# A two-layer conv / attention / mixture-of-experts trunk on one core: routing tile by tile, first expert rows by one-hot products, another order of the last experts

## What is computed

```python
grp_prob = softmax(h32 @ w_grp + b_grp)              # 4 groups
grp_p, grp_idx = top_k(grp_prob, 1)
exp_logits = (h32 @ w_exp + b_exp).reshape(T, 4, 8)
sel = take_along_axis(exp_logits, grp_idx[:, :, None], axis=1)[:, 0]
top_p, top_j = top_k(softmax(sel), 2)
gates = grp_p * top_p / sum(top_p)
experts = grp_idx * 8 + top_j
...
yb[e] = (silu(xr @ w1[e]) * (xr @ w3[e])) @ w2[e]     # xr: the rows routed to expert e
x = x + (sum over the two experts of gate * y)
```

## Time and profile before

| | us |
|---|---|
| median of 3 runs | 1643.52 (1643.09 to 1645.52) |
| the profiled execution, its own time | 1641.64 |
| its span in the trace | 1639.5 |

### The profile page before, as it was taken

How to read it: one execution, slowest core, us unless ns; L and a number is a source line. 1 busy time by engine, 2 the same in 40 slices (tenths; PEclk the granted TensorE clock), 3 DMA queues, 4 the chain that set the end, 5 groups by cost and what they waited for, 6 DMA issues and landing times.

```text
span 1639.5 us, 16522 instructions
## 1 busy us (share of the span) xinstructions
PE 1389.2 (85%) x6006; PEld 631.7 (39%) x6006; DVE 449.2 (27%) x859; ACT 329.3 (20%) x638; POOL 272.6 (17%) x373
## 2 busy tenths in 40 slices
PE   6998896988888888884799999996998888888883
PEld 3443453333332232231556666544333233223231
DVE  1898424110110110110444544425111011011012
ACT  3564230110000000000444444421100000000000
POOL 3787001121111111110000000001121111111110
PEclk9999896998999999998899999996999999999997
DMA  8322046899999999999500401226899999999994
GB/s 293 93 103 103 0 154 247 362 425 426 426 427 426 426 426 424 424 375 356 204 0 1 154 1 52 103 90 264 351 409 427 426 427 426 426 417 424 415 425 193
DMA packets 62540, 473.63 MB, mean 289 GB/s; under 512 B 15800, under 2 KB 15800, under 8 KB 36512
## 3 DMA queue, kind: packets, MB, share of 16 engines
q1 hardware_dynamic: 49792, 443.63, 65.9%
q0 software_dynamic: 10400, 16.82, 2.7%
q10 hardware_dynamic: 2304, 12.58, 2.0%
HBM read 466.95 MB, written 23.33 MB: 299 GB/s over the span
## 4 chain that ended last, share of the span: by engine, by line
PE 50%; DMA 35%; DVE 7%; POOL 2%; issue 2%; ACT 2%; SPq 1%; ACTq 0%; POOLq 0%; DVEq 0%
DMA ring<-in_moe_w 33%; PE banks L1350 19%; PE banks L1460 6%; PE banks L1296 4%; PE banks L1367 4%; PE banks L1489 3%; POOL scratch L519 2%; DVE banks L892 2%; PE banks L1209 2%; PE banks L1282 2%; PE banks L1549 2%; PE banks L1504 1%; PE banks L1229 1%; DMA area<-y_dram 1%; PE banks L1313 1%
## 5 line engine op out<-in xcount | busy, mean ns | idle before, releaser
L1350 PE MATMUL banks<-ring,scratch 128*64 128x512 f32 x1984 | 493.7, 648 | 137.7 <-DMA ring<-in_moe_w 126.8
L1350 PEld LDWEIGHTS banks<-ring,scratch 128*64 128x64 f32 x1984 | 158.4, 148 | 469.4 <-issue 469.4
L1044 DVE COPY scratch<-banks 128x256 f32<-128x256 f32 x65 | 27.6, 425 | 786.9 <-PE banks L1358 786.9
L1367 PE MATMUL banks<-ring,scratch 128*64 128x512 f32 x1008 | 230.2, 598 | 3.0 <-DVE scratch L1044 3.0
L703 ACT ACTIVATE scratch<-banks 64x512 f32<-64x512 f32 x65 | 38.3, 589 | 585.5 <-PE banks L1350 585.5
L537 POOL COPY at_out<-rows_out 128x1 int32 (+1 forms) x64 | 11.7, 183 | 685.9 <-ACT scratch L707 685.9
L1460 PE MATMUL banks<-hT,ring 128*128 128x512 f32 x256 | 117.9, 604 | 0.8 <-DVE hT L846 0.8
L1209 PE MATMUL banks<-hT,ring 128*128 128x512 f32 x256 | 113.1, 601 | 5.3 <-DMA ring<-in_conv_w_in 5.3
L1367 PEld LDWEIGHTS banks<-ring,scratch 128*64 128x64 f32 x1008 | 68.1, 136 | 117.4 <-issue 110.4
L519 POOL TENSOR_TENSOR scratch<-scratch 128x512 f32<-128x512 f32 x77 | 98.0, 1274 | 23.2 <-ACT scratch L670 12.9
L707 ACT ACTIVATE scratch<-banks 128x512 f32<-128x512 f32 x65 | 38.8, 597 | 284.3 <-PE banks L1367 284.3
(11 more groups left out here) (215 smaller groups left out, 1197.4 us busy)
## 6 DMA issues: line engine op xcount, KB each, us to landing
ring<-in_moe_w SPq DMA_DIRECT2D x187, 2048.0 KB, 20.8
area<-in_moe_w SPq DMA_DIRECT2D x6, 2048.0 KB, 12.2
ring<-in_attn_w_qkv SPq DMA_DIRECT2D x6, 2048.0 KB, 17.0
ring<-in_conv_w_in SPq DMA_DIRECT2D x4, 2048.0 KB, 14.2
area<-y_dram ACTq DMA_DIRECT2D x8, 1024.0 KB, 8.0
ring<-in_conv_w_out SPq DMA_DIRECT2D x2, 2048.0 KB, 21.2
xn_dram<-area ACTq DMA_DIRECT2D x8, 512.0 KB, 2.6
hT<-in_moe_w SPq DMA_DIRECT2D x2, 2048.0 KB, 7.7
```

The source lines that it names most:

```text
L1350: last = mm(bank[2 + s][q * SLOTS:(q + 1) * SLOTS, :], xeT[s][:, j, h, :], w[:, c, :], start=c == 0, stop=c == NC - 1)
L1367: last = mm(bank[6 + s][q * SLOTS:(q + 1) * SLOTS, :], hidT[s][:, j, :], w2c[:, j, q * 512:(q + 1) * 512], start=j == 0, stop=j == 3)
```

## The change

Five things are altered, in both layers.

1. **Raw transposes, scale afterwards.** `transpose_xn` reads x_res itself for the router, so it waits for the sum (x_done) and not for ACT's normalised rows. The factor rstd of each row and the bias (b_route, now loaded to all 128 partitions) enter on DVE, in one instruction of `choose`. The bias product of TensorE is gone.
2. **Picks tile by tile.** Within the projection's second half, transposes of tile t-1 stand behind the second of tile t's eight products, and its logits behind the third. DVE's new `choose` (16 instructions) picks a tile's experts right behind that tile's sum. Ranks are formed for tiles 0 to 2 first, then for tile 3. `stay_warm` products stand at four places.
3. **Rows of experts 0 and 1 on chip.** DVE's new `slots` makes one-hot matrices hot_first (row of a tile to slot of expert 0 or 1); TensorE multiplies xn with them, 32 products of 128x128, straight into the two banks in which the transposed rows of experts 0 and 1 are wanted. The two gathers and their 8 transposes are gone. The lists are made after that, rows_out's products (`lists2`) behind the up products of expert 0.
4. **Extra buffers.** Their order becomes area3, area2, hT, area1, so that two of them are free at the end of the projection; the fourth waits for the one-hot products, which read area1.
5. **Last experts.** The up products of expert 31 stand before the down products of 29; the weights are loaded in that order, ACT's silu and POOL's index copies (`last_scatter`) likewise. The overflow tile's first buffer comes free with down 29 and not with up 31.

```diff
@@ SP
-                to_extra(1, w2_of(1), logits_ready, l + 1)
-                to_extra(2, w1_of(3), xn_stored, 16 * NT * (l + 1))
-                to_extra(3, w3_of(3), xe_loaded[l][1], 16)
+                to_extra(1, w2_of(1), mix_ready, 8 * (l + 1))
+                to_extra(2, w1_of(3), logits_ready, NT * (l + 1))
+                sp.wait_ge(xn_stored, 16 * NT * (l + 1))
+                to_extra(3, w3_of(3), main[l]["xT_ready"], 2)
...
+                to_ring(MOE_UNITS - 5, w1_of(EXPERTS - 1), y, EXPERTS - 4)
+                to_ring(MOE_UNITS - 4, w3_of(EXPERTS - 1), up, EXPERTS - 2)
+                to_ring(MOE_UNITS - 3, w2_of(EXPERTS - 3), up, EXPERTS - 2)
                 to_ring(MOE_UNITS - 2, w2_of(EXPERTS - 2), y, EXPERTS - 3)
                 to_ring(MOE_UNITS - 1, w2_of(EXPERTS - 1), up, EXPERTS - 1)
@@ POOL
-                for s in range(2):
-                    g.indirect_dma_start(out=xe[s], out_offset=None, in_=xn_dram[l][:, :],
...
-                    scatter(e % 2, e, EXPERTS + e - 1)
+                    last_scatter(e % 2, e, EXPERTS + e - 1)
@@ DVE, add_mix
                             ins.then_inc(x_done, 1)
+                            take_hT(N_MOE[l], t)
                             invert_rms(N_MOE[l], t)
-                            if t >= 1:
-                                take_hT(N_MOE[l], t - 1)
-                take_hT(N_MOE[l], NT - 1)
+                            if t < NT - 1:
+                                choose(l, t)
@@ DVE
+            def take_first(l, s):
+                m = main[l]
+                dve.wait_ge(m["xT_ready"], 2)
+                v.tensor_tensor(xeT[s].rearrange("p j h k -> p (j h) k"), first_xT[:, :, s, :], gain_jh[N_MOE[l]],
+                                ALU.mult).then_inc(m["xT_taken"], 1)
...
+                slots(l, 0, NT - 1)
+                choose(l, NT - 1)
+                slots(l, NT - 1, NT)
@@ PE, route
+                last.then_inc(ranks_ready, 1)
+                stay_warm(1, mix_bank(l, NT))
+                logits(l, end)
+                stay_warm(4, mix_bank(l, NT))
+                pe.wait_ge(picks_done, NT * l + NT)
+                pe.wait_ge(hot_first_done, 2 * l + 1)
...
+                stay_warm(1, mix_bank(l, NT))
+
+                pe.wait_ge(xn_done, 4 * N_MOE[l] + NT)
+                pe.wait_ge(hot_first_done, 2 * l + 2)
+                for j in range(4):
+                    for h in range(2):
+                        k = 2 * j + h
+                        for t in range(NT):
+                            last = mm(bank[k // 4][:, k % 4 * P:(k % 4 + 1) * P], xn[:, t, h * 512 + j:h * 512 + j + 509:4],
+                                      hot_first[:, t].rearrange("p e s -> p (e s)"), start=t == 0, stop=t == NT - 1)
+                last.then_inc(main[l]["xT_ready"], 2)
```

## The result

The changed kernel takes **1632.18 us** (median of 8 runs, 1629.70 to 1635.36); the kernel before, on the same chips, 1643.3 (median of 8, 1640.09 to 1645.52). The ratio is 0.9934, with a 95% interval of 0.9923 to 0.9946: faster by 0.7%, 11.1 us. Forecast were 32.1 us, and 1632 lies 10 us above the range. The sign was right, the size was not: one third of the gain came.

What follows compares the result with a forecast made beforehand. The weight stream was taken to bound the kernel and to move with expert 0's start. Layers 0 and 1 before expert 0, then their ends: -14.9 - 13.3 - 2.3 - 1.6 = -32.1 us, median 1611, range 1604 to 1622.

Steps and rivals of the forecast that it cites:

- Part 1: Projection with transposes and logits between its tiles: ends 4.5 us later, picks of tiles 0 to 2 cost nothing.
- Part 2: From the projection's end to expert 0: 17.5 us at full clock, with the one-hot products at 7.14 us.
- The bounds: Limits on the one-hot products' time: 6.8 us from below, 14.3 us at half clock from above.
- the 17.5 us: Summed way from the projection's last product to expert 0's up products, at full clock, in each layer.
- The stream follows: Weight loads behind expert 0: they move with its start, with no gap and hardly a backlog.
- A: Clock falls on the way to expert 0: 1615 to 1621 with a dip (16%), 1635 in full (4%).
- B: Clock falls within the projection already, because each tile holds 2.7 us of light work: 1661; chance 2%.
- Part 3: End of the expert phases, new order and last scatter: -2.3 us in layer 1, -1.6 in layer 0.
- D: On-chip path fails to do what it says, tail gives nothing, picks slip 2 us a tile: 1623; chance 3%.

Runs made afterwards that it cites:

- e7: e5 with DVE's picks of tiles 0 to 2 made behind the projection, TensorE's part unchanged: 1647.41 us.
- e5: Changed kernel with xn written j ahead of q only ahead of the expert phases, so one-hot products and transposes of gathered rows read neighbours: 1615.24 us.
- e1: Changed kernel with step 1 in place of four floats in the one-hot products' stationary operand (features permuted): 1614.60 us.
- e10: Changed kernel with a step of two floats in the one-hot products' stationary operand (features permuted): 1614.18 us, measured one time.
- e11: Changed kernel with a step of eight floats in the one-hot products' stationary operand (features permuted): 1631.95 us, measured one time.
- e4: Changed kernel with nine more `stay_warm` products ahead of the one-hot products in both layers: 1646.83 us.
- e8: Changed kernel with rows of experts 0 and 1 gathered from DRAM again, in place of the one-hot products: 1632.18 us.
- e3: Changed kernel with the old order of the last experts, their loads and the waits that go with it: 1635.46 us.
- e9: e5 with 24 of 32 one-hot products ahead of tile 3's and lists behind expert 0's up products; result not the reference's: 1618.20 us.

## Why the prediction missed, step by step

**Part 1, the projection: right.** +4.5 forecast, +5.1 and +5.0 measured. The three logits blocks are 1.95 us where 1.71 was taken: three times 0.24. That picks of tiles 0 to 2 cost next to nothing there is borne out by e7: without them the projection's second half takes 36.74 us, with them (e5) 36.86; and moving them costs 31 us.

**Part 2: the step that failed.** "32 such products (64 records) in 7.14 us: I take that." The price of the one-hot products was taken from the earlier trace rows, whose stationary operand is contiguous; the operand of the change has a step of four floats. Measured 15.10 in place of 7.14: **+8.0 us a layer, 16 of the 22.1 us**. The bounds failed too: 14.3 us "at half clock" was the upper one, and at full clock it was 15.1. Both were built from clock and columns. No product of before loads with a step of four floats, but its transposes do (209 ns against 141, above), and the code showed the step; I did not read it as a cost. Layer 0 and 1 alike, and e1, e10 and e11 show it.

A small one in the same sum: the way from the projection's end to the one-hot products took 10.2 us (241.88 to 252.11) and not 9.45, +0.8. The logits ended 0.2 later, and `choose` took 3.87 us and not 3.3 (246.88 to 250.75), so that it ended behind the four `stay_warm` products, which the sum counted in its place (3.44). The instructions of it that carry a value per row run 0.23 to 0.27 us, not the 0.17 of the earlier trace rows.

17.5 + 8.0 + 0.8 is 26.3; 26.2 was measured. So the other terms of the 17.5 us held within 0.2, full clock among them, and e1, with the loads at 192 ns, came to 18.4.

**The stream follows: right,** by e4, e1 and the 501.2 to 502.5 us of the other runs. **Rivals A and B did not occur:** clock 1.00 over the whole way in both layers. A's times of 1615 to 1635 take in the measured one, but for another reason; the clock's rows tell the two apart.

**Part 3, the end: right in layer 1, lost in layer 0.** From expert 0's start to the last down's end it is 1.6 us shorter in layer 1 (472.1 and 470.5) and the scatter starts 0.36 us sooner behind it, -1.9 against -2.3. In layer 0, -1.6 was forecast and +1.3 measured to the first result sum, 2.9 of the 22.1 us. Part of that is the clock: TensorE runs at half clock for some of it, up 31 8.78 us where before had 7.09, the overflow tile's ups 9.52 (8.80 before) and its downs 5.06 (3.67 before). The stretch from 742 to 760 has a clock of 0.72. Each of them lies behind a wait for weights or for DVE, but the same places in e8 read 7.09, 8.78 and 3.67. Why the clock fell at the one time and not at the other, no run settles. But the clock is not all: e8, with the new order and those times, takes 501.2 us from expert 0 to that sum, only 0.7 less than before. So the -1.6 of the forecast did not come in any run; with the old order before took 501.9 and e3 504.6, and one trace of each cannot tell the order's worth in layer 0 from that spread.

**D, in a form of its own, came true:** the on-chip path did what it says and was still worth nothing against a gather (e8). I had the rival as a failure of the picks and not of the products' price.

## What to carry to other kernels

A price taken from another row holds only if the access pattern is the same too: before you take a load's or a product's time, compare the step of each operand in the code, since the profile prints shape and type but no step. If the fast reader meets a step, let an engine with time to spare lay the data out for it, at the one place where that is hidden. And what stands ahead of a saturated stream is worth its full length, in both directions: it is there that each microsecond counts. Check, though, what comes due behind it: in e9 an earlier start gained nothing, because the rows of the next expert but one were not there.

## What the runs showed of the hardware

- A 128x128 float32 weight load takes 192 ns with neighbouring elements, 196 with a step of two floats, 329 of four, 335 of eight, at full clock. Loads overlap; 64 loads with their products of 128 columns, which PEld is busy through, take 7.32, 7.71, 15.10 and 15.41 us.
- As the operand of a transpose a step costs less: the load takes 209 ns with a step of four floats (before, after) and 140 with neighbours (e5), and four transposes of gathered rows 0.68 us (after) and 0.58 to 0.60 (e5).
- ACT's 128x1024 activation takes 1.15 us in one layout and 2.15 with j ahead of q, in which it reads each eighth float.
- A narrow DVE instruction of `choose` with a value per row takes 0.23 to 0.27 us, one without 0.17 to 0.20 (after, 246.88 to 250.75).
- An indirect gather of one expert's rows took 6.42 us in e8, where the DMA share beside it was 0.71, and 9.25 and 8.36 in e9, where it was 1.01.
